# RWKV-7 recurrence: two heads on the two halves of the partitions as 64x64 TensorE tiles, in two lanes of nine turns instead of three of six

## The reference

```python
def step(state, inp):
    r_t, w_t, k_t, v_t, a_t, bb_t = inp
    sa = jnp.einsum('bhij,bhj->bhi', state, a_t)
    state = state * w_t[:, :, None, :] + sa[..., None] * bb_t[:, :, None, :] + v_t[..., None] * k_t[:, :, None, :]
    return state, jnp.einsum('bhij,bhj->bhi', state, r_t)

state, y = lax.scan(step, wkv_state.astype(f32), seq)
y = layernorm(y, ...)
out = ((y + bonus) * g)
```

## Time and profile before

| | us |
|---|---|
| median of 3 runs | 3726.37 (3725.63 to 3728.14) |
| span of the profiled execution | 3725.9 (core 0, mean granted clock 0.959) |
| feature block | 272 to 335 |
| chunk block | 335 to 597 |
| rest, from 597 | 3129 |

### The profile page before, as it was taken

The page is one execution under the profiler, slowest core; times in us unless marked ns, Lnnn a source line. Parts: engine busy times, 40 slices in busy tenths (PEclk is TensorE's granted clock), DMA queues, the critical chain, the costliest instruction groups (busy, mean ns, idle before and its releaser), DMA issues.

```text
span 3725.9 us, 33994 instructions
## 1 busy us (share of the span) xinstructions
PE 3066.2 (82%) x9408; PEld 1506.9 (40%) x9408; DVE 2662.6 (71%) x6446; ACT 1350.9 (36%) x4001; POOL 1438.4 (39%) x1241
## 2 busy tenths in 40 slices
PE   8997996988777777989898878888988877777777
PEld 5765994333232322444343433333433322322222
DVE  2676665887666667789988576899867667666664
ACT  3354221233333333324573232346633333333332
POOL 1211002454444444444345344453444344444442
PEclk9997997999899999999999999999999999999999
DMA  4100016999999999999999999999999999999998
GB/s 130 38 14 1 1 46 226 419 415 418 413 421 418 420 407 411 416 416 385 348 377 410 379 421 418 421 412 355 408 421 421 401 421 422 421 418 407 421 415 349
DMA packets 216557, 1293.13 MB, mean 347 GB/s; under 512 B 23600, under 2 KB 41008, under 8 KB 68784
## 3 DMA queue, kind: packets, MB, share of 16 engines
q0 software_dynamic: 165888, 1208.03, 79.0%
q1 hardware_dynamic: 50480, 82.93, 6.4%
HBM read 1286.49 MB, written 3.87 MB: 346 GB/s over the span
## 4 chain that ended last, share of the span: by engine, by line
DMA 42%; PE 20%; DVE 11%; issue 8%; ACT 3%; POOL 1%; DVEq 0%; SPq 0%; ACTq 0%; POOLq 0%
DMA ring<-in_uv,route 41%; PE banks L1647 15%; DVE ring L1587 4%; DVE X L1597 2%; ACT route L1632 1%; PE banks L2035 1%; PE banks L2027 1%; DVE own L2283 1%; ACT route L1617 1%; PE banks L1975 1%; PE banks L2001 1%; ACT route L1622 0%; POOL ring L1576 0%; DMA own<-in_l_peer_wq 0%; DMA own<-in_l_w_out 0%
## 5 line engine op out<-in xcount | busy, mean ns | idle before, releaser
L1647 PE MATMUL banks<-ring,route 128*128 128x512 f32 (+1 forms) x4088 | 1993.7, 624 | 553.3 <-ACT route L1632 531.7
L1576 POOL DMA_INDIRECT ring<-in_uv,route x1152 | 1322.7, 1148 | 1706.8 <-PE banks L1647 1506.0
L1587 DVE SCALAR_TENSOR_TENSOR ring<-ring,XN 128x1024 f32<-128x1024 f32 x1152 | 1408.6, 1223 | 731.5 <-DMA ring<-in_uv,route 720.0
L1647 PEld LDWEIGHTS banks<-ring,route 128*128 128x128 f32 (+1 forms) x4088 | 728.6, 189 | 1649.5 <-issue 849.0
L1617 ACT ACTIVATE route<-route 128x2 f32<-128x2 f32 x576 | 117.3, 204 | 1864.0 <-DVE ring L1587 1863.6
L1632 ACT ACTIVATE route<-IDN,route 128x128 f32<-128x128 f32 x894 | 309.3, 387 | 3.8 <-PE banks L1647 2.6
L1622 ACT ACTIVATE route<-route 128x1 f32<-128x1 f32 x1152 | 276.6, 287 | 23.2
L1975 PE MATMUL banks<-own,QP 128*128 128x512 f32 (+1 forms) x400 | 176.2, 564 | 5.3 <-DMA own<-in_l_w_in 3.1
L1597 DVE SCALAR_TENSOR_TENSOR X<-ring,route,X 128x1024 f32<-128x1024 f32 x130 | 166.4, 1280 | 0.9
L1617 ACT ACT_TABLE_LOAD x106 | 136.0, 1283 | 1.9
L1975 PEld LDWEIGHTS banks<-own,QP 128*128 128x128 f32 x400 | 76.3, 192 | 94.2 <-issue 82.0
(11 more groups left out here) (503 smaller groups left out, 3360.1 us busy)
## 6 DMA issues: line engine op xcount, KB each, us to landing
ring<-in_uv,route POOLq DMA_INDIRECT x1152
own<-in_l_w_in SPq DMA_DIRECT2D x16, 1024.0 KB
own<-in_l_w_out SPq DMA_DIRECT2D x12, 1024.0 KB
own<-in_l_peer_wq SPq DMA_DIRECT2D x12, 1024.0 KB
X<-in_x_prompt SPq DMA_DIRECT2D x8, 512.0 KB, 6.3
ring<-in_l_w_in SPq DMA_DIRECT2D x4, 1024.0 KB, 9.7
ring<-in_l_peer_wq SPq DMA_DIRECT2D x2, 2048.0 KB, 11.9
own<-in_l_w_in SPq DMA_DIRECT2D x4, 656.0 KB
```

Of the source, the lines that this page charges most:

```text
L1576: pool.indirect_dma_start(self.ring[:, s % RING, :], None, self.io[f"uv{of_slot(s)[0]}"], bass.IndirectOffsetOnAxis(ap=self.EI[:, g % 2, k ...
L1587: dve.scalar_tensor_tensor(u, u, 1.0, self.XN[:, of_slot(s)[1], :], ALU.mult, ALU.mult, accum_out=self.HD[:, g % 2, k:k + 1]).then_inc(sel ...
L1647: m = pe.matmul(self.bank[1 + half][0:n, :], self.DG[:, (V_TENSOR[s] - 1) % 4, 0:n], self.ring[:, s % RING, D + 512 * half:D + 512 * half ...
```

## The change

Heads are stacked, not put in squares: tiles are half as wide (64 columns per pair), without zeros, and every product of a pair becomes two of 64x64, the first with both operands on partitions 0 to 63, the second on 64 to 127, each writing its own partitions of the same PSUM bank. Transposes become products with a stacked identity (`stackI`). Masks are halved once, by eight POOL copies in the feature block. `blocks` and the masks of stages 0 and 1 become one operation each on 128 partitions, evacuations cover 256 columns instead of 512, `spread_v`, the zeroing and `pack` go. There are two lanes and `LAG` is 9: 90 turns, at most two chunks under way. The output weights have a buffer of their own and are loaded at the block's start. The core of the diff:

```diff
-    AR, KB, VC = big.take(NCH, 4, 2, P), big.take(NCH, 4, P), big.take(NCH, 4, 64)
-    BB = by.take(NCH, 4, P)
+    AR, KB, VC = big.take(NCH, 4, 2, 64), big.take(NCH, 4, 64), big.take(NCH, 4, 64)
+    BB = by.take(NCH, 4, 64)
+    MSI, M16, MO, M16L = by.take(2, 64), by.take(64), by.take(64), by.take(64)
+    halves = [slice(64 * h, 64 * h + 64) for h in range(2)]
...
-                pool.memset(AR[:, :, :, :, :], 0.0).then_inc(zc.h, 1)
-                pool.memset(VB[:, :, :], 0.0)
-                pool.memset(V8[:, :, :], 0.0).then_inc(zc.h, 1)
-                pool.memset(BB[:, :, :, :], 0.0).then_inc(zc.h, 1)
-                pool.memset(KB[:, :, :, :], 0.0).then_inc(zc.h, 1)
+                pool.wait_ge(cl.h, cl.at(16))
+                for q in halves:
+                    for dst, mask in ((MSI, maskSI.rearrange("p (a n) -> p a n", a=2)[q, :, q]), (M16, mask16[q, q]),
+                                      (MO, maskO[q, q]), (M16L, mask16L[q, q])):
+                        pool.tensor_copy(dst[q], mask).then_inc(mh.h, 1)
...
-                    for h in range(2):
-                        q = slice(64 * h, 64 * h + 64)
-                        o = dst[q, :, 64 * h:64 * h + 64]
-                        if scalar is None:
-                            ch.add(dve.tensor_tensor(o, a[q], b[q], ALU.mult))
-                        else:
-                            ch.add(dve.scalar_tensor_tensor(o, a[q], scalar, b[q], ALU.mult, ALU.mult))
+                    if scalar is None:
+                        ch.add(dve.tensor_tensor(dst, a, b, ALU.mult))
+                    else:
+                        ch.add(dve.scalar_tensor_tensor(dst, a, scalar, b, ALU.mult, ALU.mult))
...
                     for c in range(8):
-                        m = pe.matmul(bank[6][:, 64 * c:64 * c + 64], VB[:, c, :], stackI, start=True, stop=True)
+                        for q in halves:
+                            m = pe.matmul(bank[6][q, 64 * c:64 * c + 64], slots[VF + p][q, 64 * c:64 * c + 64], stackI[q],
+                                          start=True, stop=True)
...
-        LANES = 3
+        LANES = 2
...
-        NS, LAG, PRODUCTS = 18, 6, 17
+        NS, LAG, PRODUCTS = 18, 9, 17
...
-        def four(pe, b, lhs, rhs, n=P):
+        def four(pe, b, lhs, rhs):
             for p in range(4):
-                m = pe.matmul(b[:, p * n:(p + 1) * n], lhs[:, p, :], rhs[:, p, :], start=True, stop=True)
+                for q in halves:
+                    m = pe.matmul(b[q, p * 64:(p + 1) * 64], lhs[q, p, :], rhs[q, p, :], start=True, stop=True)
+            return m
+
+        def four_turned(pe, b, src):
+            for p in range(4):
+                for q in halves:
+                    m = pe.matmul(b[q, p * 64:(p + 1) * 64], src[q, p, :], stackI[q], start=True, stop=True)
             return m
...
+            if k in (0, 1):
                 for p in range(4):
-                    m = pe.matmul(b[k][:, p * P:(p + 1) * P], (BB, KB)[k][:, c, p, :], w.AP[:, p, :],
-                                  start=True, stop=True)
...
+                    for q in halves:
+                        m = pe.matmul(b[k][q, p * P:(p + 1) * P], (BB, KB)[k][q, c, p, :],
+                                      AR[q, c, p, :, :].rearrange("p a n -> p (a n)"), start=True, stop=True)
             elif k == 2:
...
+                four(pe, b[0], AR[:, c, :, 0, :], BB[:, c, :, :])
+                m = four_turned(pe, b[1], BB[:, c, :, :])
...
+                    o, y = b[1][:, p * 64:(p + 1) * 64], b[0][:, p * 64:(p + 1) * 64]
+                    for q in halves:
+                        pe.matmul(o[q], w.Bt[q, p, :], SA[q, p, :], start=True, stop=False)
+                    for q in halves:
+                        pe.matmul(o[q], w.Kt[q, p, :], VC[q, c, p, :], start=False, stop=True)
...
-            bc4 = lambda m: m.unsqueeze(1).broadcast_to([P, 4, P])
+            bc4 = lambda m: m.unsqueeze(1).broadcast_to([P, 4, 64])
...
+            if k in (0, 1):
+                ins = tt((w.M1, w.M2)[k], b[k].rearrange("p (q a n) -> p q a n", q=4, a=2),
+                         MSI.unsqueeze(1).broadcast_to([P, 4, 2, 64]), ALU.mult)
             elif k == 2:
...
+                dve.wait_ge(taken[lane].h, taken[lane].at(2 * count(c, 0) + 2))
+                ch(tt(w.Dg, w.M1[:, :, 0, :], bc4(M16), ALU.mult))
+                ch(tt(w.O, w.M1[:, :, 0, :], bc4(MO), ALU.mult))
+                ch(tt(w.ID, w.Dg, bc4(stackI), ALU.add))
+                ins = tt(w.Dt, v4(b[0]), bc4(M16L), ALU.mult)
...
-                through(3)
-                sp.dma_start(first_out[:, 0:4, :], wv[:, 0:4, :]).then_inc(wl[0].h, 16)
-                through(6)
-                sp.dma_start(first_out[:, 4:7, :], wv[:, 4:7, :]).then_inc(wl[1].h, 16)
+                sp.dma_start(FO[:, 0:4, :], wv[:, 0:4, :]).then_inc(wl[0].h, 16)
+                sp.dma_start(FO[:, 4:7, :], wv[:, 4:7, :]).then_inc(wl[1].h, 16)
+                sp.dma_start(first_out[7], wv[:, 7, :]).then_inc(wl[1].h, 16)
```

More of the change, by code:

```diff
@@ L785, in rwkv @@
         here, more = Room(side[:, by.at:]), Room(AF)
-        VB, V8, B8 = here.take(8, P), here.take(4, P), here.take(4, 64)
+        B8 = here.take(4, 64)
         oka, SEL = MIX[:, BT:BT + 4], MIX[:, BT + 4:]
@@ L1056, in rwkv @@
         PF = PB[:, :, :].rearrange("p f n -> p (f n)")
-        MORE = sb(s2, "chunk_more", [P, 13 * 512])
-        cut = lambda buf, n, first=0: [buf[:, first + 512 * i:first + 512 * i + 512] for i in range(n)]
-        doubles = lambda buf, first: buf[:, first:first + 1024].rearrange("p (q a n) -> p q a n", q=4, a=2)
-        more = cut(MORE, 13) + cut(side, 5, by.at) + cut(CST, 1, 832)
-        lanes = [(XF, 2560, cut(XF, 1, 4608) + more[0:9]),
-                 (PF, 0, cut(PF, 10, 2048)),
-                 (AF, 0, more[9:])]
+        FO = sb(s2, "first_weights", [P, 7, D])
+        first_out = [FO[:, k, :] for k in range(7)] + [wide[:, big.at + 256:big.at + 256 + D]]
+        cut = lambda buf, n, first=0: [buf[:, first + 256 * i:first + 256 * i + 256] for i in range(n)]
+        doubles = lambda buf, first: buf[:, first:first + 512].rearrange("p (q a n) -> p q a n", q=4, a=2)
+        lanes = [(PF, 0, cut(PF, 10, 1024)), (PF, 3584, cut(PF, 10, 4608))]
         class Work:
@@ L1070, in __init__ @@
                 self.M1 = doubles(buf, first)
-                self.M2 = doubles(buf, first + 1024)
+                self.M2 = doubles(buf, first + 512)
                 (self.Bt, self.Kt, self.Dt, self.Dg, self.O, self.ID, self.D2, self.D2T, self.W1, self.W2) = (
                     x.rearrange("p (q n) -> p q n", q=4) for x in slabs)
-                self.D4, self.D4T, self.D8T, self.AP = self.Dt, self.Dg, self.ID, self.ID
+                self.D4, self.D4T, self.D8T = self.Dt, self.Dg, self.ID
                 self.WT, self.NT = self.D2, self.D2T
-                self.YC, self.YQ = (slabs[8][:, 256 * i:256 * i + 256].rearrange("p (q n) -> p q n", q=4)
-                                    for i in range(2))
+                self.YC, self.YQ = self.W1, self.W2
                 self.b = bank[2 * lane:2 * lane + 2]
-        LANES = 3
+        LANES = 2
         work = [Work(i) for i in range(LANES)]
@@ L1148, in pe_stage @@
                 four(pe, b[0], w.D4, w.D4T)
-                for p in range(4):
-                    m = pe.transpose(b[1][:, p * P:(p + 1) * P], KB[:, c, p, :], ident)
+                m = four_turned(pe, b[1], KB[:, c, :, :])
             elif k == 7:
@@ L1153, in pe_stage @@
             elif k == 8:
-                for p in range(4):
-                    m = pe.transpose(b[1][:, p * P:(p + 1) * P], w.W1[:, p, :], ident)
+                m = four_turned(pe, b[1], w.W1)
             elif k == 9:
@@ L1170, in pe_stage @@
                 for p in range(4):
-                    o = b[0][:, p * 64:(p + 1) * 64]
-                    pe.matmul(o, AR[:, c, p, 0, :], ST[:, p, :], start=True, stop=False)
-                    m = pe.matmul(o, w.M2[:, p, 0, :], VC[:, c, p, :], start=False, stop=True)
+                    for q in halves:
+                        pe.matmul(b[0][q, p * 64:(p + 1) * 64], AR[q, c, p, 0, :], ST[q, p, :], start=True, stop=False)
+                    for q in halves:
+                        m = pe.matmul(b[0][q, p * 64:(p + 1) * 64], w.M2[q, p, 0, :], VC[q, c, p, :], start=False, stop=True)
@@ L1185, in pe_stage @@
             else:
                 pe.wait_ge(y_sig.h, y_sig.at(c + 1))
-                for p in range(4):
-                    m = pe.matmul(b[1][:, p * 64:(p + 1) * 64], YB[:, p, :], stackI, start=True, stop=True)
+                m = four_turned(pe, b[1], YB)
             m.then_inc(made[lane].h, 1)
@@ L1215, in dve_stage @@
                 roots.get(dve)
[L1216 to L1222 removed]
+                tt(YB, w.YC, ys[:, 1, :].unsqueeze(2).broadcast_to([P, 4, 64]), ALU.mult).then_inc(y_sig.h, 1)
@@ L1350, in _ @@
                     act_stage(act, c, k)
```

(4 more changed lines are left out.)

142 lines of the change are left out of this document (28 added, 114 removed).

## The result

The changed kernel takes **3686.9 us** (3685.46 to 3690.27, 4 runs) against 3726.53 (3725.63 to 3728.14) before: a ratio of 0.9892, 95% interval 0.9878 to 0.9906, 40 us faster. The forecast was 3693.

A forecast was written before the change was run, and what follows sets the result against it. TensorE was taken to bound the chunk block, whose time, like the feature block's, moves everything behind it. Chunk block 27 us less plus feature block 6 made 33: 3726.4 - 33 = 3693 us, range 3660 to 3765.

The forecast's parts named there:

- likeliest case: Chunk block: the two heads' products run beside each other, clock low now and then; total 3680 to 3705 us, chance 0.42.
- (1) Products: Chunk block: with halves side by side a 64-column record costs 0.028 us; one after the other, 0.0575.
- rival C: Chunk block: halves go one after the other and the clock holds; 31.2 us a round, total 3761, chance 0.12.
- (2) Hand-overs: Chunk block, between stages: 0.79 us through VectorE, 0.75 through ScalarE, 2.19 for stage 2; 4.26 from state sum to scaling.
- (3) The walk: Chunk block: turn-by-turn sum of one full round in two lanes, 21.0 us against 24.7.
- (4) The clock: Chunk block: a quarter of the rounds at 1.2 GHz, 31 us each; block 235 us, 27 less than 262.
- The last chunk: End of chunk block: products 5.8 us, hand-overs 12.5, first-tile products that fill waits in part, width changes; 25 us.
- (5) Feature block: Feature block: merged VectorE operations save 12.0 us, ScalarE some 6; between bounds of 2 and 10, 6 us less.
- (6) Weights: Chunk block: moving the first output tile's three weight loads to the block's start changes nothing.
- A: Chunk block: the clock holds, block 210 us, total 3668, chance 0.14.
- B: Chunk block: halves overlap only partly, 0.042 us a record, rounds near 26, total about 3724, chance 0.12.
- D: Chunk block: halves go one after the other and the clock falls; 54 us a round, total some 3955, chance 0.20.

The follow-up runs named there:

- e1: The changed kernel with, in every stage, all products of one head first and then all of the other, instead of alternating: 3774.4 us.
- e4: The changed kernel with six products (12 records) that nobody reads put on TensorE ahead of stage 17's wait: 3678.1 us.
- e6: The changed kernel with the feature block's products written again as 32 VectorE operations on 64 partitions instead of 16 on 128: 3694.3 us.
- e7: The changed kernel with the first two output-weight loads waiting for chunks 3 and 6 again: 3688.5 us.
- e2: The changed kernel with the old schedule of three lanes of six turns instead of two of nine, on the 64x64 tiles: 3647.2 us.
- e5: The changed kernel with three lanes of six turns and, in every stage, all products of one head before the other's: 3704.4 us.

## Why the prediction was right

Its likeliest case came out: 3686.9 in its own 3680 to 3705. The mechanism was right: the two halves run beside each other, and hand-overs end the turns. That the block was met to 2 us is partly luck, as two errors cancel (point 4). Point by point:

- **(1) Products.** 0.028 a record was chosen between 0.0575 and 0.028; the rows show 0.029 alternating, and e1 shows the upper end, 0.058, for the other order. This step carried the sign: e1 is the kernel after with the upper end, and it is slower than before. What the Trainium skill says of tiles in parallel (TensorEngine Tiling (Array Packing), Key Properties) is borne out by the rows at 448.31 and 448.43. Gotcha 1 of the same page of the Trainium skill (Restrictions and Gotchas), on which rival C leaned, is not: both halves write one PSUM bank in every one of these pairs, and the pairs go at 0.029 a record, half of e1's 0.058. The measurement decides.
- **(2) Hand-overs.** VectorE 0.42, ScalarE 0.38, and 4.18 us from the state sum to the scaling (454.21 to 458.39), forecast 4.26; stage 2's first product to stage 3's 3.05, in the walk 4.39 to 7.48, 3.09.
- **(3) The walk** gave 21.0 us a round at a steady clock; e4 measures 21.2. The longest wait is in front of stage 17, 2.4 us, walked as 2.7.
- **(4) The clock.** The block was forecast at 235 and is 233.3, but two errors cancel. Laid against the same marks, the prediction has 22 for the first chunk up to stage 9 and 10.7 more to its first state copy (O13's end and its hand-over stand 9.6 after O9 in the walk of 21, and a round was put at 23.5), 32.7; measured 31.0. Seven rounds of 23.5 are 164.5; measured 159.3. What is left of the last round, 12.8, and the last chunk, 25, are 37.8; measured 27.7 + 15.3 = 43.0. So the clock's term was too large: it is low for 3 to 7 us of each round rather than for all of one in four, and e4 prices that at 11 us in seven rounds, where 20 stood for eight. The 5 us put down for a slow start no run prices in two lanes.
- **The last chunk was mis-sized**, by 5 us, of which the clock is 1 (e4's round there takes 26.8 instead of 27.7). "Fill waits in part" was the step: in its middle turns TensorE doesn't wait at all. The timeline of two of these turns:

```profile
530.62 0.68 PE L1091 MATMUL banks<-CST,PB 64*64 64x64 f32 x16
531.23 1.98 PE L1260 MATMUL banks<-first_weights,X 128*128 128x512 f32 x4
...
533.15 0.68 PE L1085 MATMUL banks<-PB 64*64 64x64 f32 x16
533.76 1.98 PE L1260 MATMUL banks<-first_weights,X 128*128 128x512 f32 x4
```

A turn is 2.53 us: 0.61 for 16 quarter records that cost 0.47 elsewhere, 1.92 for four full ones that cost 4 x 0.43. The two changes of width cost 0.14 and 0.20, as forecast, but the four full records stand between the chunk's products and its next ones in the list that TensorE works through, and these turns lie on the path. A walk turn by turn, like that of the round, could have shown it.
- **(5) Feature block.** 6 forecast, 6.8 measured; e6 shows that the merged VectorE operations are 5.5 of them. The 6 was a choice between bounds of 2 and 10, not a walk, so its closeness is luck in part; that ScalarE would be the next to be late is borne out (8.5 us).
- **(6) Weights.** Nothing forecast, nothing measured (e7).
- **Not forecast:** the start is 1.5 us earlier and the rest 3.7 us shorter. All kernels with tiles have a rest of 3121 to 3126, both with squares 3128 to 3129; e7 and the kernel after, which differ in nothing there, are 3.8 apart. No run isolates a cause, and it stays open. Of the 8.3 us by which the spans differ beyond the sum's 33, these two are 5.2, the chunk block 2.3 and the feature block 0.8.
- **Rivals.** A (the clock holds, 3668): the clock does not hold. B (0.042 a record): no. C and D fall with the pace of 0.029; e1, which has their pace, gave 3774, near C's 3761 and far from D's 3955. D's second step, that a low clock would stay low through serial products, failed: in e1 it is back at 2.4 GHz for 7 to 44 us at a time. Three sums are slightly off and change nothing: by its own terms D comes to 3959, B's block of 255 to 270 to 3721 in its middle instead of 3724, and (5)'s VectorE saving to 11.8 instead of 12.0.

What the prediction did not ask is what the two lanes cost: it walked the round as given. The same walk with three lanes was not made; e2 shows where the larger gain lay.

## What to carry to other kernels

Two small products that use different rows and columns of the array pay in full only if they alternate in the instruction stream (87 us here in two lanes, 57 in three); look at the starts of the records, two at a time or one, before anything else. When products get cheaper, the hand-overs become the bound. The third chain under way was not worth more than before by that (40 us with tiles, 82 with squares), but as much as the whole change brought: take the cheaper products without giving up a lane for them. If one long idle stretch a round lets the clock fall, idle products in it pay for themselves (here 12 records, 9 us of the total); useful work moved into it should do the same, which no run here tried.

## What the hardware showed unexpectedly

- Records of one quarter of the array start ahead of records of another quarter that the program issues earlier, by about three (e1, 469.93 against 469.98 to 470.10). It makes groups of one head overlap at their ends (113 of 432 records in a round of e5), and is why e5 is faster than count times pace.
- Two 64x64 products on opposite quarters that write the same PSUM bank lose nothing: 0.029 us a record, half of 0.058.
- The clock falls within a busy block too: in the kernel after a fall to 1.2 GHz comes with the one idle stretch of 2.4 us a round, and with 12 idle records in that stretch no round from 354 us on had one. In e1 the clock is low even where TensorE is busy 19.06 of 20.50 us; why, no run isolates.
